# 48 late gate units of a gated encoder block: from plain to Strassen form, behind all branch projections

## The chip, the cores and the metric

One core of a Trainium2 chip runs the whole kernel. The metric is the device time of one execution in microseconds. TensorE does matmuls into PSUM (8 banks of 128 x 512 floats), VectorE (DVE) and ScalarE (ACT) work elementwise, GpSimd (POOL) here issues DMAs that add in DRAM, and SyncE (SP) issues most of the other DMAs.

## What is computed

One encoder layer over 512 tokens with 2048 features, in float32. Cut to what matters:

```python
xn = rms_norm(h, norm_mix_g[l])
...                                    # projections, two attentions: att_a, att_b (512 x 1024 each)
y_a = att_a @ w_branch_a[l]            # 1024 -> 2048
y_b = att_b @ w_branch_b[l]            # 1024 -> 2048
gates = jax.nn.sigmoid(xn @ w_gate[l]) # 2048 -> 4096
merged = gates[..., :D_MODEL] * y_a + gates[..., D_MODEL:] * y_b
h = h + merged @ w_out[l]
hn = rms_norm(h, norm_mlp_g[l])
u = jnp.square(jax.nn.relu(hn @ w_mlp_in[l]))
h = h + u @ w_mlp_out[l]
return rms_norm(h, norm_final_g)
```

## The kernel before

Every float32 product is made of three matmuls: each operand is split into a high part (rounded to the fast format float32r, by ScalarE) and a low part (the rest, by VectorE), and `product` adds high x high, high x low and low x high in PSUM (lines 1728 to 1730). All weights stream once from DRAM. A unit is one load of 512 KB of weights: four blocks of 128 rows by 256 columns. Its way is: SP loads it into one of four slots of `landing`, ScalarE makes `w_hi`, VectorE `w_lo` (`split`, two slots each), and TensorE multiplies (`features`, 24 matmuls of 512 columns). Semaphores count units: `unit_lo` (split), `unit_used` (multiplied).

The stages follow one another on TensorE:
- Stage 1, 88 units (UNITS1): query, key and value projections, with attention woven in, and the gates of the column blocks 0 and 1 of both branches (blocks "g" of BLOCKS), which stay in `side` as `gate`.
- Stage 2, 80 units, blocks B2 to B2_END + 1. For each column block nb of 256 (eight of them) there are four branch units (two of `w_branch_a`, two of `w_branch_b`, from at_hi and at_lo, the split attention outputs), and for six of the eight then four units each of the two gates of block nb + 2, from xn_hi and xn_lo (the split x times its gain; the division by the token's root mean square is applied to the result, by `gate_logits`). These are the 48 late gate units. VectorE multiplies gate and branch straight from PSUM (`scaled_a`, `merge_b`) and adds the two into `feat`.
- Stage 3, 32 units from B3: `w_out`, from the split merged features (`merged_part`), two banks in turn out of eight (`out_pair`).
- The up stage, 128 units in Strassen form. The operands are cut into 2 x 2 blocks and seven products replace eight: a unit is seven forms by two blocks by three matmuls of 256 columns, 42 matmuls. Four units make a group `s`, with its own four PSUM banks (`up_bank`), two groups in turn. SP loads four blocks of weights (`up_units`, laid out in DRAM as 4 KB a partition) into one of three slots `up_raw`, VectorE adds three more forms (`up_sums`), ScalarE and VectorE split the seven (`up_high`, `up_low`), and after a group VectorE mixes the seven products into four blocks (`first_product` on ScalarE, `mixed_products`, `fourth_block`, `hidden`). At step n VectorE does `up_low(n)`, what is due for older groups, and then `up_sums(n + 2)`, in this order; SP issues the load of unit n when `up_low(n - 3)` is done.
- The down stage, also in Strassen form.

Beside all this POOL runs 18 rounds of `totals`, which make sums of weight blocks in DRAM: two copies of 1 MB, two accumulating transfers of 1 MB, a copy, an accumulating transfer, a copy, an accumulating transfer, each step waiting for the one before. A round is released by `unit_used`:

```python
for m in range(2 + STEPS):
    pool.wait_ge(unit_used, 12 + 8 * m if m < 10 else 84 + 10 * (m - 9))
    for part in range(6):
        totals(m, part)
```

So rounds 10 to 17 start at units 6, 16, 26, ..., 76 of stage 2. The pair of accumulating transfers is `part == 1`.

## Time and profile before

| | |
|---|---|
| median of 3 runs | 2479.97 us (2479.5 to 2480.07) |
| span of the profiled execution | 2477.4 us; its own time is not listed, the median lies 2.6 us above the span |
| TensorE busy | 2460.5 us, 99% |
| VectorE, ScalarE, GpSimd busy | 1660.1, 1062.9, 193.0 us |
| stage 2 in the trace | from about 599 to 1032 us (80 units) |
| up stage in the trace | from about 1204 to 1847 us (128 units) |

The span runs from the first to the last instruction. TensorE's matmuls are pipelined and overlap in the records, so their mean duration (389 ns for 512 columns) is more than the distance between two of them; the distance is read from counts in a window. A landing of a DMA is the time from its issue to its semaphore. q0 is the DMA queue of POOL, q1 that of SP.

### The profile page before, as it was taken

How to read it: one execution, taken by the hardware profiler on the slowest of the kernel's cores; microseconds unless marked ns; L12 is line 12 of the kernel's file. 1: busy time of each engine (PE TensorE's matmuls, PEld its weight loads, DVE VectorE, ACT ScalarE, POOL GpSimd, SP SyncE). 2: the span in 40 equal slices, each digit the busy share in tenths (PEclk: the TensorE clock that was granted, in tenths of full speed). 3: DMA queues.
4: the chain of work that ended last, by engine and by line, in shares of the span. 5: the costliest groups of instructions: out<-in, count | busy, mean ns of one | idle time of the engine just before them, and what ended most of it. 6: DMA issues, size and time to landing. Idle time of an engine off the chain costs nothing.

```text
span 2477.4 us, 34658 instructions
## 1 busy us (share of the span) xinstructions
PE 2460.5 (99%) x14162; PEld 2176.6 (88%) x14162; DVE 1660.1 (67%) x2260; ACT 1062.9 (43%) x1382; POOL 193.0 (8%) x185
## 2 busy tenths in 40 slices
PE   9999999999999999999999999999999999999998
PEld 8898898898888888888999999999998888888886
DVE  6566555556333332544788888888869788877898
ACT  5566755556222222312433433333335444444445
POOL 0011000100010100101200000000001011110010
PEclk9999999999999999999999999999999999999999
DMA  7788998888898999965554434433479666566652
GB/s 262 212 254 240 237 250 244 234 251 224 231 263 246 245 251 254 257 181 151 167 191 153 135 131 131 134 128 130 135 230 336 229 230 225 190 225 232 233 191 108
DMA packets 226819, 517.11 MB, mean 209 GB/s; under 512 B 30672, under 2 KB 159840, under 8 KB 215152
## 3 DMA queue, kind: packets, MB, share of 16 engines
q1 hardware_dynamic: 213712, 363.52, 44.1%
q0 software_dynamic: 12672, 151.00, 24.3%
q8 instruction: 103, 1.69, 0.3%
q10 hardware_dynamic: 288, 0.54, 0.1%
q14 instruction: 44, 0.36, 0.0%
HBM read 489.80 MB, written 176.20 MB: 269 GB/s over the span
## 4 chain that ended last, share of the span: by engine, by line
PE 95%; DVE 3%; ACT 1%; issue 1%; DMA 0%; SPq 0%; ACTq 0%; DVEq 0%
PE bank L1728 31%; PE bank L1730 30%; PE bank L1729 30%; PE bank L1803 1%; PE bank L1838 1%; PE bank L1817 1%; DVE ring L1519 0%; DMA stream<-in_x_features 0%; DVE up_lo L1411 0%; DVE form_lo_b L1377 0%; DVE stream L1547 0%; DVE stream L1568 0%; DVE at_lo L1261 0%; ACT q_twice L752 0%; DVE stream L1559 0%
## 5 line engine op out<-in xcount | busy, mean ns | idle before, releaser
L1045 DVE TENSOR_TENSOR w_lo<-landing,w_hi 128x1024 fp32r<-128x1024 f32 x199 | 247.7, 1244 | 447.4 <-ACT w_hi L696 447.3
L1728 PE MATMUL bank<-xn_hi,w_hi 128*128 128x512 f32 x1184 | 464.7, 392 | 2.3 <-DVE w_lo L1202 1.3
L1730 PE MATMUL bank<-xn_hi,w_lo 128*128 128x512 f32 x1184 | 461.2, 390 | 0.0
L1729 PE MATMUL bank<-xn_lo,w_hi 128*128 128x512 f32 x1184 | 460.7, 389 | 0.0
L696 ACT ACTIVATE w_hi<-landing 128x1024 fp32r<-128x1024 f32 x199 | 210.9, 1060 | 575.6 <-PE bank L1730 575.2
L919 ACT ACTIVATE up_hi<-up_raw 128x1792 fp32r<-128x1792 f32 x128 | 218.1, 1704 | 401.8 <-PE bank L1730 391.5
L968 ACT ACTIVATE ring<-down_raw 128x1024 fp32r<-128x1024 f32 x224 | 237.5, 1061 | 312.4 <-PE bank L1730 312.4
L1519 DVE TENSOR_TENSOR ring<-down_raw,ring 128x1024 fp32r<-128x1024 f32 x224 | 285.4, 1284 | 68.2 <-ACT ring L968 68.0
L1411 DVE TENSOR_TENSOR up_lo<-up_raw,up_hi 128x1792 fp32r<-128x1792 f32 x128 | 259.9, 2030 | 85.2 <-ACT up_hi L919 85.2
L1728 PEld LDWEIGHTS bank<-xn_hi,w_hi 128*128 128x128 f32 x1184 | 222.4, 188 | 47.3 <-issue 3.3
L1730 PEld LDWEIGHTS bank<-xn_hi,w_lo 128*128 128x128 f32 x1184 | 222.2, 188 | 46.9
L1729 PEld LDWEIGHTS bank<-xn_lo,w_hi 128*128 128x128 f32 x1184 | 222.5, 188 | 44.9 <-issue 0.2
L1728 PE MATMUL bank<-ring,down_forms 128*128 128x512 f32 x656 | 255.5, 390 | 0.9 <-DVE ring L1519 0.9
L1729 PE MATMUL bank<-ring,down_forms 128*128 128x512 f32 x656 | 255.2, 389 | 0.0
L1730 PE MATMUL bank<-ring,down_forms 128*128 128x512 f32 x656 | 255.2, 389 | 0.0
L1728 PE MATMUL bank<-form_hi_b,up_hi 128*128 128x256 f32 x896 | 253.8, 283 | 0.4 <-DVE up_lo L1411 0.4
L1728 PE MATMUL bank<-form_hi_a,up_hi 128*128 128x256 f32 x896 | 253.6, 283 | 0.0
L1730 PE MATMUL bank<-form_hi_b,up_lo 128*128 128x256 f32 x896 | 253.6, 283 | 0.0
L1729 PE MATMUL bank<-form_lo_a,up_hi 128*128 128x256 f32 x896 | 253.6, 283 | 0.0
L1729 PE MATMUL bank<-form_lo_b,up_hi 128*128 128x256 f32 x896 | 253.6, 283 | 0.0
L1730 PE MATMUL bank<-form_hi_a,up_lo 128*128 128x256 f32 x896 | 253.6, 283 | 0.0
L1728 PEld LDWEIGHTS bank<-form_hi_b,up_hi 128*128 128x128 f32 x896 | 172.0, 192 | 0.7 <-DVE up_lo L1411 0.6
(192 smaller groups left out, 4386.4 us busy)
## 6 DMA issues: line engine op xcount, KB each, us to landing
down_totals<-in_down_blocks POOLq DMA_DIRECT2D x64, 1024.0 KB, 9.4
up_raw<-in_up_units SPq DMA_DIRECT2D x128, 512.0 KB, 3.4
down_raw<-down_totals SPq DMA_DIRECT2D x128, 512.0 KB, 4.4
down_raw<-in_down_blocks SPq DMA_DIRECT2D x96, 512.0 KB, 4.3
landing<-in_w_in SPq DMA_DIRECT2D x71, 512.0 KB, 6.2
landing<-in_w_gate SPq DMA_DIRECT2D x64, 512.0 KB, 6.3
landing<-in_w_out SPq DMA_DIRECT2D x32, 512.0 KB, 3.7
hidden_rows<-hidden_out SPq DMA_DIRECT2D x32, 512.0 KB, 3.4
```

What stands on the lines that cost most here:

```text
L696: nc.scalar.activation(w_hi[:, u % SPLIT, :], landing[:, u % LAND, :], ACT.Copy).then_inc(unit_hi, 1)
L919: nc.scalar.activation(up_hi[n % 2], up_raw[n % 3][:, 1:8, :], ACT.Copy).then_inc(up_hi_done, 1)
L968: nc.scalar.activation(ring[i % RING][:, 0, :], raw_of(i), ACT.Copy).then_inc(piece_hi, 1)
L1045: nc.vector.tensor_tensor(w_lo[:, s, :], landing[:, u % LAND, :], w_hi[:, s, :].bitcast(F32), ALU.subtract).then_inc(unit_lo, 1)
L1411: nc.vector.tensor_tensor(up_lo[n % 2], up_raw[n % 3][:, 1:8, :], up_hi[n % 2].bitcast(F32), ALU.subtract).then_inc(up_lo_done, 1)
L1519: nc.vector.tensor_tensor(part[:, 1, :], raw_of(i), part[:, 0, :].bitcast(F32), ALU.subtract)\
L1728: nc.tensor.matmul(dst, a_hi, b_hi, start=start, stop=False, **kw)
L1729: nc.tensor.matmul(dst, a_hi, b_lo, start=False, stop=False, **kw)
L1730: return nc.tensor.matmul(dst, a_lo, b_hi, start=False, stop=stop, **kw)
L1803: ins = nc.tensor.matmul(bank[:, bk, col:col + n], query[:, t * P:(t + 1) * P], keys[:, first:first + n], start=col == 0 and k == 0, stop= ...
L1817: ins = nc.tensor.transpose(bank[:, bk, col + k * P:col + (k + 1) * P], probs[:, start + k * P:start + (k + 1) * P], identity[:])
L1838: ins = nc.tensor.matmul(dst, v_parts[:, s, j, head, :], moving, start=j == 0 and part is pt_hi, stop=j == TT - 1 and part is pt_lo, skip_ ...
```

## The change

All 32 branch units come first, the 16 of branch a and then the 16 of branch b. Products of the column blocks 0 and 1 are multiplied by their gates as before (`scaled_a`, `merge_b`). Those of the six later blocks are kept (`keep_branch` on ScalarE): y_a in `feat`, y_b through two buffers into DRAM (`store_yb`), from where it comes back block by block (`load_yb`). Meanwhile x is loaded again, scaled by gain and root mean square, and made into the seven Strassen forms for each of eight feature pairs (`x_form_block`, `x_form_sums`, `x_form_high`, `x_form_low`), in three batches, the last of which waits for the end of the branch units. Then the 48 gate units run as 12 groups of four in the form of the up stage, with three slots `gate_raw`. After a group ScalarE applies the sigmoid (`open_gate`) and VectorE multiplies with y_a (even groups) or with y_b, and adds (odd groups, `through_gate`). The first w_out unit gets split buffers of its own, and three splits and the merged parts move. POOL's rounds 13 to 17 are released by gate units. The diff, cut to its core:

```diff
+KEPT = 2
+GROUPS = 2 * (D // CB - KEPT)
+GATE_UNITS = 4 * GROUPS
+GATE_ORDER = (list(IN_TURN) + [(s, v) for s in range(2, GROUPS - 2) for v in range(4)]
+              + [(GROUPS - 2 + s, v) for s, v in IN_TURN])
+X_BATCHES = (range(0, 4), range(4, 6), range(6, 8))
...
+            def load_x_forms(batch):
+
+                kps = X_BATCHES[batch]
+                sp.wait_ge(unit_used, UNITS1 + (0, BRANCH_UNITS // 2, BRANCH_UNITS)[batch])
+                for kp in kps:
+                    for i in (kp, kp + KP):
+                        slots = slice(0, 8, 7) if i < KP else slice(3, 7, 3)
+                        sp.dma_start(x_raw[kp][:, slots, :], x_blocks[:, i, :].rearrange("p (h n) -> p h n", h=2))\
+                            .then_inc(x_form_landed[batch], 16)
+
+            def store_yb(nb):
+
+                sp.wait_ge(yb_kept, nb - KEPT + 1)
+                sp.dma_start(yb_rows[nb - KEPT], yb_stage[nb % 2]).then_inc(yb_stored[nb % 2], 16)
+
+            def load_yb(nb):
+
+                if nb == KEPT:
+                    sp.wait_ge(yb_stored[0], 16 * 3)
+                sp.wait_ge(merged, nb)
+                sp.dma_start(yb_back[:], yb_rows[nb - KEPT]).then_inc(yb_landed, 16)
+
+            def load_gate(n):
+
+                s, v = GATE_ORDER[n]
+                if n == 0:
+                    sp.wait_ge(att_ready, HEADS)
+                elif n < 3:
+                    sp.wait_ge(unit_lo, UNITS1 + BRANCH_UNITS - 4 + 2 * n)
+                else:
+                    sp.wait_ge(gate_lo_done, n - 2)
+                sp.dma_start(gate_raw[n % 3][:, 0:4, :].rearrange("p b n -> p (b n)"),
+                             gate_units[s % 2 * (D // CB) + KEPT + s // 2, v]).then_inc(gate_landed[n % 3], 16)
+
+            for w in range(BRANCH_UNITS):
+                src, nb = (wba, wbb)[w // 16], w % 16 // 2
+                load(B2 + w // 4, w % 4, src[:, KU * (w % 2):KU * (w % 2 + 1), nb * CB:(nb + 1) * CB], CB)
+                if w == 6:
+                    load_x_forms(0)
+                elif w == 20:
+                    load_gate(0)
+                elif w == 22:
+                    load_x_forms(1)
+                elif w in (27, 29, 31):
+                    store_yb((w - 23) // 2)
+            load_gate(1)
+            load_gate(2)
+            load_x_forms(2)
+            for n in range(3, GATE_UNITS):
+                load_gate(n)
+                if n in (3, 4, 5):
+                    store_yb(n + 2)
+                for s in range(1, GROUPS, 2):
+                    if n == min(gate_end(s) + 2, GATE_UNITS - 1):
+                        load_yb(KEPT + s // 2)
...
+            def keep_branch(q):
+
+                m, nb = q // 8, q % 8
+                if nb < KEPT:
+                    return
+                act.wait_ge(unit_used, UNITS1 + 2 * q + 2)
+                bank_pair = bank[:, 2 * (nb % 2):2 * (nb % 2) + 2, :]
+                if m == 0:
+                    nc.scalar.activation(feat[:, 2 * nb:2 * nb + 2, :], bank_pair, ACT.Copy).then_inc(ya_kept, 1)
+                    return
+                if nb < 4:
+                    act.wait_ge(merged, KEPT)
+                else:
+                    act.wait_ge(yb_stored[nb % 2], 16 * (nb // 2 - 1))
+                nc.scalar.activation(yb_stage[nb % 2], bank_pair, ACT.Copy).then_inc(yb_kept, 1)
...
+            def gate_high(n):
+
+                act.wait_ge(gate_summed, 3 * n + 3)
+                if n == 0:
+                    act.wait_ge(merged, KEPT)
+                elif n == 1:
+                    act.wait_ge(unit_used, UNITS1 + BRANCH_UNITS)
+                else:
+                    act.wait_ge(gate_used, n - 1)
+                nc.scalar.activation(gate_hi[n % 2], gate_raw[n % 3][:, 1:8, :], ACT.Copy).then_inc(gate_hi_done, 1)
...
+            def open_gate(s):
+
+                act.wait_ge(gate_mixed, 5 * s + 5)
+                nc.scalar.activation(gate_mix[:, 0:4, :], gate_mix[:, 0:4, :], ACT.Sigmoid).then_inc(gate_open, 1)
+
+            act.wait_ge(at_lo_done, KB // 2)
+            for w in range(2, BRANCH_UNITS):
+                split(B2 + w // 4, w % 4)
+                if w >= 3 and w % 2 == 1:
+                    keep_branch((w - 3) // 2)
+                if 12 <= w < 16:
+                    x_form_high(w - 12)
+                elif w in (26, 27):
+                    x_form_high(w - 22)
+
+            for n in range(GATE_UNITS):
+                gate_high(n)
+                if n == 1:
+                    keep_branch(15)
+                elif n in (2, 3):
+                    x_form_high(n + 4)
+                if n >= 4 and GATE_ORDER[n - 4][1] == 3:
+                    open_gate(GATE_ORDER[n - 4][0])
+                if n >= 2 and GATE_ORDER[n - 2][1] == 3:
+                    gate_first_product(GATE_ORDER[n - 2][0])
...
+            def x_form_block(kp):
+
+                batch = x_batch(kp)
+                dve.wait_ge(x_form_landed[batch], 16 * 2 * len(X_BATCHES[batch]))
...
+            def through_gate(s):
+
+                nb = KEPT + s // 2
+                dve.wait_ge(gate_open, s + 1)
+                if s % 2 == 0:
+                    dve.wait_ge(ya_kept, nb - KEPT + 1)
+                    nc.vector.tensor_tensor(feat_blocks(nb), feat_blocks(nb), gate_blocks, ALU.mult).then_inc(gated, 1)
+                    return
+                dve.wait_ge(yb_landed, 16 * (nb - KEPT + 1))
+                nc.vector.tensor_tensor(gate_blocks, gate_blocks, yb_blocks, ALU.mult).then_inc(branch_b, 1)
+                dve.wait_ge(branch_b, nb + 1)
+                dve.wait_ge(gated, s // 2 + 1)
+                nc.vector.tensor_tensor(feat_blocks(nb), feat_blocks(nb), gate_blocks, ALU.add)\
+                    .then_inc(merged, 1)
+                dve.wait_ge(merged, nb + 1)
...
+            for n in range(GATE_UNITS):
+                gate_low(n)
+                if n == 1:
+                    x_form_block(6)
+                    x_form_block(7)
+                    x_form_sums(2)
+                elif n in (3, 4):
+                    x_form_low(n + 3)
+                if n >= 4 and GATE_ORDER[n - 4][1] == 3:
+                    through_gate(GATE_ORDER[n - 4][0])
+                if n >= 2 and GATE_ORDER[n - 2][1] == 3:
+                    mixed_gate(GATE_ORDER[n - 2][0])
+                if n >= 3 and GATE_ORDER[n - 3][1] == 3:
+                    fourth_gate(GATE_ORDER[n - 3][0])
+                if n + 2 < GATE_UNITS:
+                    gate_sums(n + 2)
...
+            fourth_gate(GROUPS - 2)
             merged_part(0)
-            split(B2_END, 2)
             merged_part(1)
-            split(B2_END, 3)
-            scaled_a(B2_END, 0, NBR - 2)
+            split(B3, 0)
             merged_part(2)
...
+            merged_part(3)
+            through_gate(GROUPS - 2)
+            mixed_gate(GROUPS - 1)
+            fourth_gate(GROUPS - 1)
+            split(B3, 1)
...
             for m in range(2 + STEPS):
-                pool.wait_ge(unit_used, 12 + 8 * m if m < 10 else 84 + 10 * (m - 9))
+                if m < 13:
+                    pool.wait_ge(unit_used, 12 + 8 * m if m < 10 else 84 + 10 * (m - 9))
+                else:
+                    pool.wait_ge(gate_used, (4, 14, 25, 36, 47)[m - 13])
...
+            def gate_unit(n, s, v):
+
+                pe.wait_ge(gate_lo_done, n + 1)
+                if v == 0 and s == 0:
+                    pe.wait_ge(att_ready, HEADS)
+                elif v == 0 and s == 1:
+                    pe.wait_ge(yb_kept, 6)
+                elif v == 0:
+                    pe.wait_ge(gate_mixed, 5 * (s - 1))
```

## Rows read from the trace of the kernel before

**Rows 1.** The page: span, busy shares, granted clock, the chain that ended last.

```profile
span 2477.4 us, 34658 instructions
PE 2460.5 (99%) x14162; PEld 2176.6 (88%) x14162; DVE 1660.1 (67%) x2260; ACT 1062.9 (43%) x1382; POOL 193.0 (8%) x185
...
PE 95%; DVE 3%; ACT 1%; issue 1%; DMA 0%; SPq 0%; ACTq 0%; DVEq 0%
```

**Rows 2.** Waits of TensorE: whole span's longest, then all from 590 to 1260 us.

```profile
PE bank L1728 <- DVE w_lo L1202: 1.3, 1, 1.3
...
PE bank L1728 <- DVE up_lo L1411: 0.4, 1, 0.4
PE bank L1728 <- DVE w_lo L1045: 0.2, 1, 0.2
```

**Rows 3.** Windows: length, busy (count) of PE, PEld, DVE, ACT, POOL; clock, DMA share, GB/s.

```profile
744.00:806.00 62.00, 62.00 (x275) 51.32 (x274) 18.48 (x16) 13.79 (x13) 6.88 (x10) 1.00 0.88 250
1426.00:1488.00 62.00, 62.00 (x519) 62.00 (x518) 54.04 (x75) 24.80 (x24) 0.00 (x0) 1.00 0.40 131
```

**Rows 4.** Timeline of SP: start, length, issues; 795 to 828 and 638 to 650.

```profile
797.90 27.47 SPq L501 DMA_DIRECT2D landing<-in_w_gate  x6
...
640.06 5.86 SPq L501 DMA_DIRECT2D landing<-in_w_branch_a  x2
```

**Rows 5.** Timeline of ScalarE in the up stage: two splits.

```profile
1406.25 1.70 ACT L919 ACTIVATE up_hi<-up_raw 128x1792 fp32r<-128x1792 f32 x1 [2.73 <-PE bank L1730]
...
1411.29 1.70 ACT L919 ACTIVATE up_hi<-up_raw 128x1792 fp32r<-128x1792 f32 x1 [2.73 <-PE bank L1730]
```

**Rows 6.** Timeline at the start of stage 2: VectorE, ScalarE, TensorE.

```profile
604.18 4.62 DVE L1261 TENSOR_TENSOR at_lo<-stream,at_hi 128x1024 fp32r<-128x1024 f32 x4
...
606.38 1.04 ACT L696 ACTIVATE w_hi<-landing 128x1024 fp32r<-128x1024 f32 x1
...
609.99 0.50 PE L1728 MATMUL bank<-at_hi,w_hi 128*128 128x512 f32 x1 [0.21 <-DVE w_lo L1045]
```

**Rows 7.** Timeline of VectorE in the up stage: low part, mixing, sums, low part.

```profile
1413.03 2.02 DVE L1411 TENSOR_TENSOR up_lo<-up_raw,up_hi 128x1792 fp32r<-128x1792 f32 x1 [1.50 <-ACT up_hi L919]
1414.97 0.68 DVE L1425 TENSOR_TENSOR mix<-bank,first_term 128x512 f32<-128x512 f32 x1
...
1417.09 0.68 DVE L1400 TENSOR_TENSOR up_raw<-up_raw 128x512 f32<-128x512 f32 x1
...
1418.60 2.02 DVE L1411 TENSOR_TENSOR up_lo<-up_raw,up_hi 128x1792 fp32r<-128x1792 f32 x1
```

**Rows 8.** Landings: landing 620 to 1054 us; up_raw; the load of 645.55.

```profile
DMA to landing us min/median/max: 3.3/5.9/13.3
...
DMA to landing us min/median/max: 3.1/3.4/7.9
...
landing<-in_w_branch_a SPq DMA_DIRECT2D x1, 512.0 KB, 12.4
```

**Rows 9.** DMA queues by window (packets, MB, share): 650:653; 656:659; 667:672; 1410:1415 us.

```profile
q0 software_dynamic: 74, 0.57, 91.4%
q1 hardware_dynamic: 75, 0.08, 9.3%
...
q1 hardware_dynamic: 998, 0.99, 99.3%
...
q1 hardware_dynamic: 16, 0.02, 1.2%
...
q1 hardware_dynamic: 144, 0.52, 30.1%
```

**Rows 10.** Timeline of POOL in round 10: trigger, accumulating pair, third accumulating transfer.

```profile
632.38 1.01 POOL L1663 DMA_DIRECT2D down_totals<-in_down_blocks  x2 [20.65 <-PE bank L1730]
641.17 1.74 POOL L1666 DMA_DIRECT2D down_totals<-in_down_blocks  x2 [7.77 <-DMA down_totals<-in_down_blocks]
...
664.95 0.80 POOL L1666 DMA_DIRECT2D down_totals<-in_down_blocks  x1 [7.03 <-DMA down_totals<-down_totals]
```

More of the change, by code:

```diff
@@ L92, in up_place, with gate_end, x_batch @@
     return UP_ORDER.index((s, v))
+def gate_end(s):
+    return GATE_ORDER.index((s, 3))
+def x_batch(kp):
+    return next(b for b, kps in enumerate(X_BATCHES) if kp in kps)
 def summed_in_dram(n):
@@ new lines, in x_form_block @@
+            def x_form_block(kp):
+                batch = x_batch(kp)
+                dve.wait_ge(x_form_landed[batch], 16 * 2 * len(X_BATCHES[batch]))
+                for i in (kp, kp + KP):
+                    slots = slice(0, 8, 7) if i < KP else slice(3, 7, 3)
+                    nc.vector.scalar_tensor_tensor(
+                        out=x_raw[kp][:, slots, :], in0=x_raw[kp][:, slots, :], scalar=gains[:, 0, i:i + 1],
+                        in1=rms_row[:].rearrange("p (h n) -> p h n", h=2), op0=ALU.mult, op1=ALU.mult)\
+                        .then_inc(x_form_raw, 1)
@@ new lines, in _ @@
+            for w in range(2, BRANCH_UNITS):
+                split(B2 + w // 4, w % 4)
+                if w in (3, 5):
+                    scaled_a((w - 3) // 2)
+                elif w in (19, 21):
+                    merge_b((w - 19) // 2)
+                if 8 <= w < 12:
+                    x_form_block(w - 8)
+                elif w == 12:
+                    x_form_sums(0)
+                elif 13 <= w < 17:
+                    x_form_low(w - 13)
+                elif w in (24, 25):
+                    x_form_block(w - 20)
+                elif w == 26:
+                    x_form_sums(1)
+                elif w in (27, 28):
+                    x_form_low(w - 23)
+                elif w == 30:
+                    gate_sums(0)
@@ L1381, in _ @@
                 for u in range(KU):
[L1382 to L1384 removed]
+                    if n or u == 3:
+                        split(B3 + n, u)
+                    if n == 0 and u == 2:
                         merged_part(NBR - 1)
@@ L1879, in gate_block @@
-            def gate_block(b, pair, left):
-                pe.wait_ge(branch_b if pair else branch_a, left)
-                for u in range(4):
-                    features(b, u, 2 * pair, KU * u, u == 0, u == 3, xn_hi, xn_lo)
-            with pe.Fori(0, LOOP2) as i:
-                for j in range(2):
-                    b = i * PER2 + (B2 + 3 * j)
-                    nb = i * 2 + j
-                    branches(b, nb)
-                    gate_block(b + 1, 0, nb + 1)
-                    gate_block(b + 2, 1, nb + 1)
@@ L1892, in _, with branch @@
-            branches(B2_END, NBR - 2)
-            pe.wait_ge(branch_a, NBR - 1)
-            for u in range(2):
-                features(B2_END + 1, u, 0, KU * u, u == 0, u == 1, at_hi, at_lo)
-            pe.wait_ge(branch_b, NBR - 1)
-            for u in range(2):
-                features(B2_END + 1, 2 + u, 2, KB // 2 + KU * u, u == 0, u == 1, at_hi, at_lo)
+            def branch(w):
+                m, nb, half = w // 16, w % 16 // 2, w % 2
+                pe.wait_ge(at_lo_done, 4 * m + 2 * half + 2)
+                if half == 0 and m == 0 and nb < KEPT:
+                    pe.wait_ge(scaled_ready, N_BLOCKS1 - 1 + nb)
+                elif half == 0 and nb < KEPT:
+                    pe.wait_ge(ya_kept, 5 + nb)
+                elif half == 0 and nb < 4:
+                    pe.wait_ge((branch_a, branch_b)[m], nb - 1)
+                elif half == 0:
+                    pe.wait_ge((ya_kept, yb_kept)[m], nb - 3)
+                features(B2 + w // 4, w % 4, 2 * (nb % 2), KU * half, half == 0, half == 1, at_hi[m], at_lo[m])
```

325 lines of the change are left out of this document (203 added, 122 removed).

## The prediction

> **What bounds the kernel now.** I read the page first: TensorE is busy in 2460.5 of 2477.4 us at its full clock, and the chain that ended last is 95% TensorE [rows 1]. The view of waits then says that this busy time is nearly free of holes: from 590 to 1260 us, which holds all the work that the change touches, TensorE waits twice, 0.6 us in all [rows 2]. So the time is the number of matmuls times their pace, and the question is what the new form gives back in pace and what it newly makes TensorE wait for. The windows give both paces: in a stretch of branch and gate units 62 us hold 275 matmuls of 512 columns (225.5 ns each), in the up stage, whose form the change copies, 62 us hold 519 of 256 columns (119.5 ns) [rows 3]. DVE is the other thing to see there: 18.5 of 62 us in the gate stretch, 54.0 in the up stage. VectorE goes from idle to nearly the bound.
>
> **The gain.** A gate unit before is 24 matmuls of 512 columns. SP issues one load per unit: six issues span 27.47 us, less the issue's own 0.37, over five gaps: 5.42 us a unit [rows 4]. In the new form a unit is 42 matmuls of 256 columns; ScalarE's splits of the up stage start every 5.04 us [rows 5]. 48 units x 0.38 us = 18.2 us less, if none waits. (From the paces [rows 3] it is 18.9; I take the spacings, where no missing record counts.) The 32 branch units only change order.
>
> **Entry into the stage.** ScalarE now waits for all of at_lo before it splits branch unit 2. Before, it split at 606.38, and at_lo ended at 608.80; VectorE's half followed at once and TensorE resumed at 609.99 [rows 6]. Now: 608.85 + 1.04 (ScalarE's row) + 1.2 (VectorE, 4.62 for four of this size), about 611.1. Cost 1.2 us with the handoffs. The moved branch units, scaled_a, merge_b and the copies that keep a branch have two bank pairs in turn and ScalarE and VectorE mostly idle beside them (13.8 and 18.5 of 62 us [rows 3]); stores of y_b (512 KB, bound by the loads' 3.3 to 13.3 us to landing [rows 8]) have two units or more each. I cost these at nothing; without that cover a unit's copy would be some 1.1 us. The x loads are wanted four units later at the least.
>
> **Steady pace of the gate groups.** From the up stage [rows 5, 7], with S the start of a unit on TensorE (where ScalarE's split starts): ScalarE splits the next unit S to S+1.70, VectorE subtracts S+1.74 to S+3.7, and TensorE wants it at S+5.04, so the slack is about 1.3 us. VectorE's effective costs (start to start) are 1.94 for the low part, 1.52 for the three sums, 2.12 for the four mixing steps. The heaviest new step, an odd group's passage through its gate, has two dependent operations over 1024 columns, 1.16 each back to back [rows 6], which I set at 2.5 us with the waits between and behind them: 1.94 + 2.5 + 1.52 = 5.96, and the next subtraction starts 0.9 late, inside the slack. So the pace holds, when data are there.
>
> **Start of the gate stage.** Call E the end of the last branch unit. The last forms of x (features 6 and 7) take memory that the branches read until E, so SP issues their four loads (1 MB) at E, and VectorE stands at them before it comes to unit 2. If nothing else is moving they land about E+6 (four issues of 0.4, then the 2 us of lead and 3.1 us for 1024 packets at the 333 a microsecond that q1 reaches alone: 998 packets in 3 us [rows 9]). Behind them: four products and four sums of 128x512 (0.68 each and a handoff, 2.8 and 2.8), the three sums of unit 3 (1.52), the subtraction (2.0): 9.1 us [rows 7]. Unit 2 then starts at E+15.1 where TensorE wants it at E+10.1: 5.0 us. But a round of POOL's totals is running: its trigger is 6 units before E, and its third accumulating transfer starts 32.6 us after the trigger (632.38 to 664.95), which is E [rows 10]. For five microseconds such a transfer leaves q1 next to nothing (16 packets) [rows 9]; with that the loads land near E+9 and the hold-up is 8 to 9. ScalarE's chain (it waits for a store of y_b queued behind those loads, then 1.06 + 1.70) ends about E+15 and is covered by VectorE's. I take 7.5, bounds 5 and 10.
>
> **POOL's rounds against a shorter lead.** This is the largest term, and the least certain. Before, a unit's load had four landing slots; now it has three and VectorE must reach it one step earlier, for the sums. Load n is issued when the subtraction of unit n-3 ends, at S(n-4)+3.85; behind its landing stand sums 1.52 and the subtraction of unit n-1, 2.0, due at S(n-4)+15.1. So a landing may take 7.7 us without cost; beyond, TensorE waits the difference. In the up stage landings are 3.4 (median; POOL quiet); in the gate stage of before 3.3 to 13.3 [rows 8]. The long ones have a pattern: POOL's two accumulating transfers at 641.17 held up the load issued at 645.55 for 12.4 us, until 658.0, 25.5 after the trigger at 632.38 [rows 4, 8, 10]. It starves for 4 us, then its 1 KB packets go one for one with POOL's 8 KB packets, 75 against 74 in 3 us, until POOL is done [rows 9]. The new loads come in 4 KB packets (144 for 0.52 MB in 5 us of the up stage [rows 9]), 128 instead of 512, so one for one they need about 5 to 6 us: first packet at 17.5, landed at about 24.1 after the trigger. The rounds keep their triggers (gate units 4, 14, 25, 36, 47, at a unit's start), and the load that falls into the gap is issued at trigger + 10.1 + 3.85 = 13.9: 10.2 us to landing, 2.5 over the 7.7. In the rounds at 4 and 36 a load of y_b (512 KB more) is queued ahead of it: 1.4 us more, 3.9. Four rounds (that of unit 47 meets w_out's loads, four slots): 2.5 + 2.5 + 3.9 + 3.9 = 12.8. After such a hold-up VectorE has no slack left, and a heavy step next to it costs again: in round one the step with a passage, a mixing and sums (1.94 + 1.2 + 2.12 + 1.52 = 6.8 against 5.04) 1.7, in round two an odd passage 0.9: 2.6, taken as 2.5. The term is 15.3 us; its bounds are 0 (landings under 7.7) and 21 (landed as late as before's: 25.5 - 13.9 = 11.6, 3.9 over, with the y_b load ahead 5.3: 2 x 3.9 + 2 x 5.3 + 2.5).
>
> The Trainium skill ("DMA: Bandwidth & Descriptors", section "Queues, rings and completion order") says that each DMA engine takes turns between its queues packet by packet; the 75 against 74 agree. By that rule the size of packets decides, which speaks for 10.2 rather than 11.6. It doesn't enter the sum otherwise.
>
> **End of the gate stage.** VectorE has after the last subtraction: mixing, fourth block, seven merged parts, passage and mixing of the last group, three splits. Counted from the start of unit 46, out unit 1 gets its split at 16.8 (3.7 low part, 2.12 + 0.4, four merged parts and a split at 1.14, passage 1.14, mixing 2.1 and 0.4, split 1.14), wanted at 10.1 + 5.4 = 15.5: 1.3 us. The first and third out units are ready in time.
>
> **Sum.** -18.2 + 1.2 + 7.5 + 15.3 + 1.3 = +7.1 us on the profiled span 2477.4. The span lies 2.6 below the median of the runs, which I carry over: 2479.97 + 7.1 = 2487.1, slower by 0.29%.
>
> **Rivals.**
> 1. *Landings under 7.7 us (other side).* 4 KB packets get through POOL's, or the load that matters just misses the two transfers. The rounds cost nothing, the start 5: -18.2 + 1.2 + 5 + 1.3 = -10.7, 2469.3. For it: the up stage's 3.4 with the same packets. Against: there POOL moves nothing; and 4 us pass before even the first packet. It decides at 7.7 us of landing in the four rounds. With the start at 7.5 it is 2471.8. Chance 0.30.
> 2. *Half of it.* Landings of 9: 1.3 us in a round, 5 in all, start 7.5, no second step: -3.2, 2476.8; up to 2483 with the second steps. No measurable change. Chance 0.17.
> 3. *Worse: landings as before's, or a clock that falls.* The rounds at 21, the start at 9: +14.3, 2494.3. And the longest wait of TensorE that the view lists is 1.3 us [rows 2]; now it would wait 7.5. The granted clock is 1.00 [rows 3], the 2.4 GHz level. Were it to fall to 1.2 GHz after the five hold-ups, with half a unit lost each time (2.5 us, an estimate from the 5.04 of [rows 5]), 12.5 us come on top of the forecast: 2499.6. Chance 0.12. The Trainium skill ("TensorE: Matmul & The Clock Gate", section "Why this matters for your kernels") warns that gaps of idleness between bursts bring the half clock; no row here shows it either way.
> 4. *The forecast*, 2481 to 2494: chance 0.41.
>
> That the new form doesn't save time on TensorE isn't open: the pace of both forms is measured side by side.
>
> **Range and chances.** Nothing under 0.2% (5 us) can be told from no change. Slower by more: the forecast, its lower edge cut off, and rival 3: 0.52. Faster: 0.29. Between: 0.19. The range runs from just under rival 1 to between rival 3's two prices, 2468 to 2497; the forecast's own is 2481 to 2494.
>
> **What would show it.** Right: in windows of the gate stage without a hold-up 42 matmuls per 5.04 us; TensorE waits on gate_lo after unit 1 (5 to 10 us, VectorE at x_raw's products waiting for a DMA), and once in each round, at units 9, 19, 30 and 41, 2 to 4 us, with VectorE's sums released by the DMA into gate_raw; a longest landing of gate_raw near 10. Wrong: gate_raw landings all under 8, a stage without waits, or waits that follow mixing or passage steps without a late landing, which would mean that VectorE is the bound. What I trust least is how 4 KB packets share with POOL's.

## The result, and the profile after

The changed kernel takes 2516.36 us (median of 4 runs, 2512.95 to 2519.13) against 2479.73 (2478.96 to 2480.07) beside it: the ratio is 1.0148, 95% interval 1.0134 to 1.0163. It is slower by 1.48%, 36.6 us, where 7.1 were forecast and the range ended at 2497. The page of the profiled run, with the lines that answer to [rows 1]; the lines under its first two are the chain that ended last, by engine and by line:

```profile
span 2511.1 us, 36310 instructions
PE 2456.8 (98%) x15026; PEld 2212.7 (88%) x15026; DVE 1817.5 (72%) x2488; ACT 1119.4 (45%) x1414; POOL 193.5 (8%) x185
...
PE 84%; DVE 7%; DMA 5%; ACT 1%; issue 1%; SPq 0%; DVEq 0%; ACTq 0%
PE bank L2017 27%; PE bank L2019 27%; PE bank L2018 27%; DMA gate_raw<-in_gate_units 4%; DVE gate_lo L1511 2%; PE bank L2092 1%; PE bank L2127 1%; PE bank L2106 1%; DVE gate_raw L1501 1%; DMA stream<-in_x_features 0%; DMA x_raw_c<-in_x_features 0%; DVE ring L1805 0%; DVE up_lo L1697 0%; DVE gate_raw L1504 0%; ACT gate_hi L1019 0%
```

TensorE's busy time hardly moved, the span grew by 33.7 us, and 4% of the chain is now the transfer into gate_raw, where transfers had rounded to 0 (a transfer's whole flight counts in the chain, work beside it too, so this isn't yet the loss). The waits say the same from both sides: first TensorE's longest over the whole span (total, times, longest; [rows 2] had one of 1.3 and next to nothing around the gate), then, from 590 to 1080 us, what VectorE and ScalarE stood at:

```profile
PE bank L2017 <- DVE gate_lo L1511: 34.3, 15, 10.9
PE bank L2017 <- DVE w_lo L1231: 2.5, 3, 1.5
...
DVE gate_raw L1501 <- DMA gate_raw<-in_gate_units: 53.5, 17, 5.7
ACT gate_mix L1003 <- DMA yb_rows<-gate_mix: 12.8, 1, 12.8
...
DVE x_raw_c L1471 <- DMA x_raw_c<-in_x_features: 8.2, 1, 8.2
```

TensorE waits for the low part of a gate unit 15 times. VectorE, which makes it, was held 17 times by a load (line 1501 is the first of a unit's three sums). TensorE's 10.9 us are the start of the stage; its other 14 waits, 23.4 us, are what VectorE's slack leaves of the 53.5 that it stood at loads.

Windows of the gate stage (columns as in [rows 3]):

```profile
790.00:810.00 20.00, 13.23 (x89) 13.23 (x90) 17.05 (x19) 9.50 (x7) 0.92 (x2) 0.69 0.63 171
810.00:830.00 20.00, 19.74 (x165) 19.54 (x163) 16.39 (x22) 6.93 (x6) 2.63 (x4) 1.00 0.94 285
830.00:850.00 20.00, 16.52 (x121) 16.14 (x122) 14.63 (x20) 7.10 (x6) 1.34 (x2) 0.91 0.84 213
...
890.00:910.00 20.00, 17.19 (x131) 16.99 (x130) 15.11 (x19) 6.64 (x6) 1.85 (x3) 0.91 0.82 226
...
1010.00:1030.00 20.00, 18.38 (x138) 18.18 (x137) 14.02 (x19) 5.50 (x5) 1.32 (x2) 0.90 0.91 246
```

At full pace (42 in 5.04 us) such a window would hold 167 matmuls; 165 are in the second, 121 and 131 in others. The granted clock shows a second loss, 0.69, 0.91, 0.91, 0.90: it falls behind the longer waits. Where each microsecond went comes out of TensorE's timeline, counting 42 matmuls to a unit from the start of each. Gap is the extra time ahead of a unit's first matmul:

```
stage: unit 0 at 775.7, unit 2 at 796.77 (gap 11.1), unit 47 at 1061.46, end 1066.5
gaps at unit: 8 0.6, 9 3.3, 12 1.5, 15 1.3, 19 3.0, 25 3.0, 28 0.7, 29 3.1, 30 0.4,
              36 0.9, 38 4.1, 40 1.8, 43 1.1, 44 0.8, 46 0.7      (others 5.04 a unit)
half clock:   796.77-802.47 (26 matmuls, 0.213 us apart behind the first), 840.05-843.45 (16), 898.16-901.36 (15),
              932.23-935.62 (16), 1009.06-1014.12 (23)
```

From unit 2 to unit 47 pass 264.7 us where 45 x 5.04 is 226.8: 37.9 too many. The five half-clock stretches are 20.8 us long and hold 96 matmuls, which take 11.5 at 0.1195: 9.3 lost. The listed gaps make 26.3, and smaller ones the rest, 2.3. With the start the account closes: -18.2 (gain) + 11.1 + 37.9 + 1.3 + 0.4 (two gaps among the branch units) + 0.9 (end) = 33.4 of 33.7.

### The profile page after: what moved, and what is told of

It is laid out like the page before. It is cut to its first block, busy times and chain, and to the rows that moved or that the text cites. A ratio compares the mean times of both kernels' runs of the same rounds, so it can differ in the third digit from the quotient of the medians.

```text
span 2511.1 us, 36310 instructions
## 1 busy us (share of the span) xinstructions
PE 2456.8 (98%) x15026; PEld 2212.7 (88%) x15026; DVE 1817.5 (72%) x2488; ACT 1119.4 (45%) x1414; POOL 193.5 (8%) x185
## 4 chain that ended last, share of the span: by engine, by line
PE 84%; DVE 7%; DMA 5%; ACT 1%; issue 1%; SPq 0%; DVEq 0%; ACTq 0%
PE bank L2017 27%; PE bank L2019 27%; PE bank L2018 27%; DMA gate_raw<-in_gate_units 4%; DVE gate_lo L1511 2%; PE bank L2092 1%; PE bank L2127 1%; PE bank L2106 1%; DVE gate_raw L1501 1%; DMA stream<-in_x_features 0%; DMA x_raw_c<-in_x_features 0%; DVE ring L1805 0%; DVE up_lo L1697 0%; DVE gate_raw L1504 0%; ACT gate_hi L1019 0%
## 5 line engine op out<-in xcount | busy, mean ns | idle before, releaser
L1231 DVE TENSOR_TENSOR w_lo<-landing,w_hi 128x1024 fp32r<-128x1024 f32 x150 | 187.4, 1250 | 248.6 <-ACT w_hi L835 248.5
L835 ACT ACTIVATE w_hi<-landing 128x1024 fp32r<-128x1024 f32 x150 | 158.9, 1059 | 374.1 <-PE bank L2019 363.7
L2017 PE MATMUL bank<-xn_hi,w_hi 128*128 128x512 f32 x792 | 312.4, 394 | 3.0 <-DVE w_lo L1387 1.3
L2019 PE MATMUL bank<-xn_hi,w_lo 128*128 128x512 f32 x792 | 308.8, 390 | 0.0
L2018 PE MATMUL bank<-xn_lo,w_hi 128*128 128x512 f32 x792 | 308.3, 389 | 0.0
L2017 PEld LDWEIGHTS bank<-xn_hi,w_hi 128*128 128x128 f32 x792 | 148.8, 188 | 33.5 <-issue 4.4
L2019 PEld LDWEIGHTS bank<-xn_hi,w_lo 128*128 128x128 f32 x792 | 148.7, 188 | 31.7
L2018 PEld LDWEIGHTS bank<-xn_lo,w_hi 128*128 128x128 f32 x792 | 148.9, 188 | 29.6 <-issue 0.2
L2017 PEld LDWEIGHTS bank<-form_hi_a,up_hi 128*128 128x128 f32 x896 | 172.0, 192 | 0.8 <-DVE up_lo L1697 0.8
```

What stands on the lines that cost most here:

```text
L835: nc.scalar.activation(hi, landing[:, u % LAND, :], ACT.Copy).then_inc(unit_hi, 1)
L1231: nc.vector.tensor_tensor(lo, landing[:, u % LAND, :], hi.bitcast(F32), ALU.subtract).then_inc(unit_lo, 1)
L2017: nc.tensor.matmul(dst, a_hi, b_hi, start=start, stop=False, **kw)
L2018: nc.tensor.matmul(dst, a_hi, b_lo, start=False, stop=False, **kw)
L2019: return nc.tensor.matmul(dst, a_lo, b_hi, start=False, stop=stop, **kw)
```

## The experiments

Each was timed beside the kernel of before on the same chip; ratios are against that kernel, whose medians there were 2479.62 (first four), 2479.21 (next four) and 2479.14 (last four). The changed kernel was timed apart from them, so a difference from it is taken between what each has over its own kernel of before (36.6 us for the change).

### POOL's late rounds left out, in both kernels

POOL runs 18 rounds of block totals for the down stage; rounds 12 to 17 lie beside the gate stage. Both kernels leave them out, and down steps 10 to 15 read plain blocks in place of those sums, so nothing else moves.

```diff
-                src = down_blocks[m // 2, m % 2, BLOCK_OF[j]] if j in BLOCK_OF else down_totals[m // 2, m % 2, SUM_OF[j]]
+                src = down_blocks[m // 2, m % 2, {**BLOCK_OF, **SUM_OF}[j]] if j in BLOCK_OF or m >= 10 else down_totals[m // 2, m % 2, SUM_OF[j]]
...
-            sp.wait_ge(totals_added, 16 * 4 * (2 + STEPS))
+            sp.wait_ge(totals_added, 16 * 4 * 12)
...
-            for m in range(2 + STEPS):
+            for m in range(12):
```

(The edit is the same in both kernels.)

> The changed kernel with POOL's rounds 12 to 17 left out (the down stage reads plain weight blocks in place of the sums of steps 10 to 15, so that part of the computation is changed, with the same bytes). Theory 1 (POOL's transfers make the loads late, lateness makes TensorE wait, waits lower its clock): the 25.8 us of waits behind unit 2 in the gate stage go down to under 3, the half-clock stretches behind them (four, 6.7 us lost) vanish, landings of gate_raw stay under 7; the start still waits, for 1 MB of x, some 5 to 9 us instead of 11.1, with one half-clock stretch. Time 2470 to 2476. Rival (VectorE is the bound of the gate stage: its steps with mixing and passage don't fit into 5.04 us): waits at the heavy steps stay, 10 us or more behind unit 2, time over 2490.

> Control: the kernel before with the same rounds 12 to 17 left out (same change of the computation). If what the left-out rounds cost before is nothing, as its view of waits says (0.6 us of waits in this stage), the time stays within 1 us of 2479.7. Should it fall by several us as well, the gain of the run above isn't the gate stage's alone.

The changed kernel took 2474.16 us (2472.59 to 2477.75, 10 runs), ratio 0.9979 [0.9969, 0.9989]. The one of before took 2479.45, ratio 0.9999 [0.999, 1.0009]. The same six rounds cost the new form 42.2 us and the old one 0.2. TensorE's waits for the low part, the landings of gate_raw, and the windows, without the rounds:

```profile
PE bank L2017 <- DVE gate_lo L1511: 6.2, 2, 5.4
...
DMA to landing us min/median/max: 3.4/3.7/14.1
...
790.00:810.00 20.00, 18.58 (x140) 18.58 (x141) 16.94 (x18) 8.37 (x6) 0.00 (x0) 0.86 0.41 118
810.00:830.00 20.00, 20.00 (x168) 19.99 (x168) 17.05 (x22) 8.09 (x8) 0.00 (x0) 1.00 0.45 136
```

168 matmuls in 20 us are four units of 5.0: the gain is there. What stays is unit 2 (gap 5.6, then 18 matmuls at half clock, 791.42 to 795.42), and unit 10, 0.9 late, where VectorE meets a passage, a mixing and sums in one step. So VectorE is not the bound, and the loss comes with the rounds. That they cost the form with four landing slots next to nothing points at the lead that loads now have; the runs below try that.

### Unread matmuls keep the clock up

The changed kernel, with matmuls whose results nobody reads ahead of six waits: 85 before unit 2, 24 each before units 9, 19, 25, 29 and 38.

```diff
+                for _ in range({2: 85, 9: 24, 19: 24, 25: 24, 29: 24, 38: 24}.get(n, 0)):
+                    nc.tensor.matmul(up_products(s if n > 2 else 0, 7, 8)[:, 0, :], x_hi[0][:, 0, 0:P],
+                                     x_hi[0][:, 0, :], start=False, stop=False, skip_group_check=True)
                 pe.wait_ge(gate_lo_done, n + 1)
```

> The changed kernel with matmuls that nobody reads (256 columns each, into the unused eighth half bank) ahead of the waits of units 2 (85 of them), 9, 19, 25, 29 and 38 (24 each), so that TensorE works through most of each long wait. Theory 1: the waits end when they did, the five stretches at 1.2 GHz (20.8 us long, 9.3 us lost) vanish, time 2505 to 2510. Rival (the slow stretches are not due to idleness, or the time is anyway given by the loads and VectorE, so a faster clock is only waited away): 2513 or more.

2515.89 us (2512.68 to 2525.01), ratio 1.0158 [1.0138, 1.0177]: no gain, as the rival had it. Yet the mean clock went from 0.992 to 0.997 and the stretches at half clock from five to two (799.03 to 802.40 and 976.62 to 979.82). The window of the second hold-up has full clock now:

```profile
830.00:850.00 20.00, 17.30 (x140) 16.73 (x140) 14.53 (x20) 7.38 (x6) 1.34 (x2) 1.00 0.75 207
```

From unit 3 to unit 47 it took 255.3 us against 257.1. The rival's reason, that a faster clock is only waited away, is not shown by this, because the unread matmuls had a price of their own. They were set for the waits of one execution, and in this one two of those waits were short or missing. At unit 25 (VectorE's timeline, then TensorE's):

```profile
928.53 2.02 DVE L1511 TENSOR_TENSOR gate_lo<-gate_raw,gate_hi 128x1792 fp32r<-128x1792 f32 x1
...
929.67 3.04 PE L2174 MATMUL bank<-x_hi_a 128*128 128x256 f32 x24
932.55 0.28 PE L2017 MATMUL bank<-x_hi_a,gate_hi 128*128 128x256 f32 x1
```

The low part was ready at 930.5 and TensorE came to it at 932.55, 2.0 late; ahead of unit 38 it was ready before the 24 began, and they cost 2.9. These 4.9 us are about what the clock gave back behind unit 2: one stretch that loses 1.5 us instead of four that lose 6.7. And unit 2's gap grew from 11.1 to 14.1 us, since here a load into gate_raw came late as well. So whether the clock's 9.3 us could be had in the changed kernel stays open.

### The start of the stage alone

Two stores of y_b and the load of unit 3 go ahead of the x loads, and the forms of features 6 and 7 are made behind unit 3.

```diff
             load_gate(2)
+            store_yb(5)
+            load_gate(3)
+            store_yb(6)
             load_x_forms(2)
-            for n in range(3, GATE_UNITS):
+            for n in range(4, GATE_UNITS):
...
-                if n == 1:
+                if n == 3:
                     x_form_block(6)
                     x_form_block(7)
                     x_form_sums(2)
```

> The changed kernel with the start of the gate stage in another order: stores 5 and 6 of y_b and the load of unit 3 ahead of the x loads of the last batch, and that batch's products and sums on VectorE behind the low part of unit 3 instead of unit 1. Theory 1 with two chains at the start (VectorE behind the x loads, ScalarE behind a store of y_b, the second 1.7 us shorter): the 11.1 us before unit 2 go to under 2, new waits of 2 to 4 us come before units 4 and 5, no half-clock stretch at the start: 8 us less, 2505 to 2511. Rival (the start is bound by VectorE's work, which is only moved): 2513 to 2517.

2513.35 us (2505.83 to 2514.17), ratio 1.0136 [1.0119, 1.0153], some 3 us below the change, with intervals that overlap: the rival's range. The profiled execution was the fastest of the four, 2505.83. In it unit 2 has no wait, but units 4, 5 and 7 have 3.6, 0.9 and 3.2 of it, the first and the last with half clock behind them. From the start of the stage to unit 8 it takes 52.4 us instead of 54.6. So most of the start's cost is only moved, and 2.2 us of it are saved; the rest of that execution's lead came later, from unit 8 to unit 47 (226.0 us instead of 231.3), where nothing was changed.

### The rounds moved into the down stage

Nothing is left out. Rounds 12 to 17 run one by one behind the block sums of the odd down steps 1 to 11, and SP waits for a step's totals before it loads them.

```diff
+                if m % 2 == 1 and 12 + m // 2 < 2 + STEPS:
+                    for part in range(6):
+                        totals(12 + m // 2, part)
...
                 sp.wait_ge(piece_lo, i - RAW_SLOTS + 1)
+                if p == 0:
+                    sp.wait_ge(totals_added, 16 * 4 * (m + 3))
                 load_raw(i)
```

> The changed kernel, all work kept, with POOL's rounds 12 to 17 moved into the down stage (one behind the block sums of each odd step from 1 to 11; SP waits for the round of a step before its first load). Theory 1: the gate stage looks as with the rounds left out (2474.2), and the down stage, whose loads have twelve slots, hides the rounds: 2472 to 2478. Rival: the down stage's own loads (SP's queue 190 GB/s there) collide with the rounds and TensorE waits for piece_lo: 2485 or more.

2473.71 us (2470.82 to 2476.97, 10 runs), ratio 0.9977 [0.9968, 0.9987]: the same as without the rounds, and 42 us below the changed kernel. The down stage takes them for nothing, though its 16 DMA engines are then busy to 0.94 and 0.99 (0.65 and 0.64 in the same windows of before); these windows of it have no hole on TensorE:

```profile
1900.00:2000.00 100.00, 100.00 (x443) 82.81 (x442) 86.88 (x86) 52.33 (x51) 24.35 (x17) 1.00 0.94 314
2100.00:2200.00 100.00, 100.00 (x443) 82.81 (x442) 79.86 (x81) 45.15 (x45) 17.82 (x16) 1.00 0.99 338
```

So this much traffic doesn't cost TensorE anything by itself. The down ring has 12 landing slots, gate_raw three, which fits the lead as what decides; the two stages differ in more than that, and a fourth slot for gate_raw was not tried.

### More lead for the loads: the sums one step later

The sums of a unit stand one step later in VectorE's order, which gives a landing one unit more. Run on the changed kernel, with the other start, and with the other start and the moved rounds.

```diff
                 gate_low(n)
+                if n >= 2 and n + 1 < GATE_UNITS:
+                    gate_sums(n + 1)
...
-                if n + 2 < GATE_UNITS:
-                    gate_sums(n + 2)
+                if n == 0:
+                    gate_sums(2)
```

> The changed kernel with VectorE's three sums of a unit one step later (behind the low part of unit n come the sums of unit n + 1, not of n + 2), rounds where they were. The late load then blocks nothing until one unit later: by the prediction's working the landing that costs nothing rises from 7.7 to about 12 us. Theory 1 with the lead as the weak point: the landings stay (longest near 10.7), but the 25.8 us of waits behind unit 2 fall to under 6, only the start stays: 2487 to 2496. Rival (the DMA engines' throughput is the bound, whatever the order): waits move to other units, 2508 or more.

> The run before with the start in its other order as well (stores 5 and 6 and the load of unit 3 ahead of the x loads, the last forms of x behind unit 3). Theory 1: the start's 11 us go down to 3 to 6, in pieces short enough to keep the clock: 2480 to 2489. Rival (start's cost is only moved): as the run before.

> All three: rounds moved to the down stage, sums one step later, start in its other order. Theory 1: only VectorE's own work at the start is left (1 to 4 us), with 1.7 at the entry and 1 at the end: 2479.7 - 18.2 + 4 to 7 = 2465 to 2469. Rival (a floor of VectorE in the gate stage shows once the loads are in time): 2472 or more.

2501.70 us (2497.94 to 2504.97), ratio 1.0086 [1.0069, 1.0103]; with the start 2495.76 (1.0069 [1.0052, 1.0086]); with all three 2489.54 (1.0040 [1.0026, 1.0055]). All three lie above what I had expected (2487 to 2496, 2480 to 2489, 2465 to 2469). VectorE's waits for the loads from 800 to 1060 us, in the first of them, have nearly gone:

```profile
DVE gate_lo L1511 <- ACT gate_hi L1019: 42.0, 29, 1.8
DVE gate_raw L1501 <- DMA gate_raw<-in_gate_units: 5.3, 3, 2.4
```

The rounds are the same, and one unit more of lead takes these waits away: that is the runs' best evidence for the lead, though the units also come slower now. The first line is what took their place, and the last expectation missed it. VectorE's and ScalarE's timeline of the third kernel, in a step with nothing else to do:

```profile
864.47 2.02 DVE L1517 TENSOR_TENSOR gate_lo<-gate_raw,gate_hi 128x1792 fp32r<-128x1792 f32 x1 [0.63 <-ACT gate_hi L1024]
866.41 0.68 DVE L1507 TENSOR_TENSOR gate_raw<-gate_raw 128x512 f32<-128x512 f32 x1
868.05 1.70 ACT L1024 ACTIVATE gate_hi<-gate_raw 128x1792 fp32r<-128x1792 f32 x1 [3.61 <-DVE gate_raw L1512]
869.78 2.02 DVE L1517 TENSOR_TENSOR gate_lo<-gate_raw,gate_hi 128x1792 fp32r<-128x1792 f32 x1 [1.77 <-ACT gate_hi L1024]
```

Low part (1.94), sums of the next unit (1.64), its split (1.73) and the next low part now form one ring: 5.31 us a unit, 0.27 over TensorE's 5.04. Steps with a mixing or a passage take longer still (5.6 and 6.0 us from one low part to the next), so that units 8 to 47 take 5.49 us each. A kernel further down differs from this one in the sums alone (the other start with the rounds moved, 2470.22): the later sums cost 19.3 us there, more than the 18.2 that the new form gains. Where the rounds stay they are still worth having (14 us).

### Smaller packets in POOL's accumulating transfers

If packets take turns, POOL's of 4 KB instead of 8 should let the loads through sooner.

```diff
-    accum_op=ALU.add, max_dma_last_dim=8192
+    accum_op=ALU.add, max_dma_last_dim=4096
```

> The changed kernel with POOL's accumulating transfers cut into packets of at most 4 KB instead of 8 KB, nothing else. Theory 1 with turns packet by packet: a gate load of 128 packets of 4 KB that goes one for one with them loses half as much to them; the longest landings of gate_raw fall from 10.7 to about 8 to 9, the waits behind unit 2 from 25.8 to 10 to 15 us, time 2500 to 2508. Rival (what counts is the time until the first packet, some 4 us, or the bytes queued by POOL, not the size of a packet): landings stay at 10 to 11, time within 3 us of 2516.4.

2510.77 us (2506.71 to 2513.42), ratio 1.0127 [1.0111, 1.0142]: 5 us better than the change, with intervals that just overlap, between the expectations. Longest landing and median are 13.2 and 6.1 (14.3 and 6.3), and the long waits came at units 2, 20, 31 and 41 instead. Behind the start the longest landings are 12.4 to 12.9 us, where the change has 10.4 to 10.8: they didn't fall to 8 or 9, as theory 1 had it. What this says of turn-taking stays open.

### What is left, with the rounds moved

Three kernels on top of the moved rounds: 45 unread matmuls ahead of unit 2; the other start; and that start with ScalarE's wait for all of at_lo put off from branch unit 2 to unit 8.

```diff
-            act.wait_ge(at_lo_done, KB // 2)
             for w in range(2, BRANCH_UNITS):
                 split(B2 + w // 4, w % 4)
+                if w == 7:
+                    act.wait_ge(at_lo_done, KB // 2)
```

> The kernel with the rounds moved to the down stage (2473.7), with 45 unread matmuls of 256 columns ahead of the wait of unit 2. There the wait of 5.7 us is the stage's only long one and 4 us at 1.2 GHz follow it. Theory 1: the stretch vanishes, unit 2 lasts 5.04 instead of 7.2 us, and as no late load follows, all of the 1.8 to 2.2 us is gained (2471.7, at the edge of what the runs tell; the profile shows it). Rival, as the unread matmuls in the changed kernel showed: it is waited away behind the next units and the start of unit 10 relative to the stage's start is the same.

> Rounds moved to the down stage and the start in its other order, sums where they were (two units ahead). Theory 1, after the run in which sums one unit ahead closed a ring of 1.94 + 1.52 + 1.75 = 5.3 us: units keep 5.04 us, the start costs about 4 instead of 5.7 + 2: 2470 to 2472. Rival (the other order fits only with late sums): 2474 or more.

> As the run before, and ScalarE waits for at_lo only ahead of its first write into feat (behind the split of branch unit 7) instead of ahead of that of unit 2. Theory 1: the 1.5 us of wait at branch unit 2 goes, 2469 to 2471; if it was hidden anyway, the same as the run before.

The unread matmuls: 2470.76 us (2469.95 to 2471.57), ratio 0.9966 [0.9953, 0.9979], some 3 less than the moved rounds, with intervals that overlap; the profile is the better witness. TensorE's first matmul of unit 2 there:

```profile
791.27 0.39 PE L2019 MATMUL bank<-x_hi_a,gate_hi 128*128 128x256 f32 x1 [0.39 <-DVE gate_lo L1513]
791.49 0.28 PE L2020 MATMUL bank<-x_lo_a,gate_hi 128*128 128x256 f32 x1
791.61 0.28 PE L2021 MATMUL bank<-x_hi_a,gate_lo 128*128 128x256 f32 x1
791.73 0.28 PE L2019 MATMUL bank<-x_hi_a,gate_hi 128*128 128x256 f32 x1
```

0.12 apart from the second on; unit 2 lasts 5.14 us and not 7.23, and from unit 3 to unit 47 both kernels take 223.0. So here, with nothing to wait for behind it, the 2 us of the clock can be had. The other start: 2470.22 (2469.63 to 2471.81), ratio 0.9965 [0.9952, 0.9979]; it removes the wait at unit 2, gets one of 2.8 at unit 4 and the half clock behind it (28 matmuls, 798.19 to 804.33). The last: 2469.46 (2468.73 to 2470.20), ratio 0.9961 [0.9947, 0.9975]. The gap at the entry is 0.69 us instead of 1.90. It is the fastest kernel here: 9.7 us below before, 46 below the change; its interval overlaps those of the two runs ahead of it.

## Why the prediction was wrong

**Direction and mechanism held.** The gate stage has its gain of 0.38 us a unit wherever a unit has its data; TensorE waits on gate_lo after unit 1 and then for loads that met POOL's pairs, at units 9, 19, 29 and 40 (forecast 9, 19, 30 and 41) for 3.3, 3.0, 3.1 and 1.8 us (2.5 or 3.9 each), 11.2 in all where 12.8 were forecast. Those loads landed about when it was worked out that they would. Two answers on DMA issues of the changed kernel, from 824 to 826.5 and from 859 to 861.5 us (last number: us to landing):

```profile
gate_raw<-in_gate_units SPq DMA_DIRECT2D x1, 512.0 KB, 10.8
...
gate_raw<-in_gate_units SPq DMA_DIRECT2D x1, 512.0 KB, 9.5
```

The first is a load that meets the pair: 10.8 (10.4, 10.6 and 10.5 in the next three rounds) against 10.2. And the queues of 888 to 889 us (packets, MB, share):

```profile
q0 software_dynamic: 20, 0.16, 78.5%
q1 hardware_dynamic: 19, 0.08, 20.5%
```

One for one with POOL's packets, as the 1 KB packets did in [rows 9], and 4 KB each. What I had trusted least was right. That 10.2 came so near is luck in part: a first packet at 17.5 and 5 to 6 us of packets make 22.5 to 23.5 after the trigger, 8.6 to 9.6 to landing, and no row stands for the rest of the way to 24.1. In the round of 867.8 the first packet came 18.2 after the trigger, and it took 7.8 more to landing.

**The step that failed** is the term "POOL's rounds", 15.3 us with a bound of 21. Behind unit 2's own stretch (2.6 us) it measured 35.3: 28.6 of gaps and 6.7 of half clock. It priced one load in each round, the one that meets the pair, and took every other accumulating transfer and copy at nothing. The loads that it priced cost 11.2 of the 26.3 us of listed gaps; the other 15.1, with 2.3 of small gaps and the 6.7 of half clock, it did not have (1.3 of all this is there without the rounds too). The second row above is such a load: issued beside a single accumulating transfer, it landed after 9.5 us. Nine loads from unit 3 on were issued up to 4 us behind the start of a single one, and took 6.8 to 10.4 us, five of them 8.0 or more, over the 7.7 that a landing may take. The longest wait behind the start, 4.1 us at unit 38, came from neither: its load was issued at 994.6, together with the two copies that open a round, and took 10.7. VectorE's timeline and POOL's put it side by side:

```profile
829.64 0.42 DVE L1540 TENSOR_TENSOR gate_mix<-bank,gate_mix 128x256 f32<-128x256 f32 x1
835.01 0.69 DVE L1501 TENSOR_TENSOR gate_raw<-gate_raw 128x512 f32<-128x512 f32 x1 [4.96 <-DMA gate_raw<-in_gate_units]
...
870.10 0.69 DVE L1501 TENSOR_TENSOR gate_raw<-gate_raw 128x512 f32<-128x512 f32 x1 [3.44 <-DMA gate_raw<-in_gate_units]
...
893.33 0.69 DVE L1501 TENSOR_TENSOR gate_raw<-gate_raw 128x512 f32<-128x512 f32 x1 [4.57 <-DMA gate_raw<-in_gate_units]
```

```profile
819.76 1.72 POOL L1952 DMA_DIRECT2D down_totals<-in_down_blocks  x2 [8.85 <-DMA down_totals<-in_down_blocks]
...
857.64 0.81 POOL L1952 DMA_DIRECT2D down_totals<-in_down_blocks  x1 [5.33 <-DMA down_totals<-down_totals]
```

The pair of 819.76 holds VectorE until 835.01 (TensorE 3.3), the single transfer of 857.64 holds it until 870.10 (TensorE 1.3). VectorE stood at a load 17 times, not four. The trace of before had it to be seen. Asked one by one, 20 of its loads from 620 to 1000 us took 8.1 us or more, and the longest of all met no pair: it was issued at 901.18 behind a single accumulating transfer, and the next pair came when it had landed (POOL, the landing, POOL):

```profile
897.95 0.81 POOL L1666 DMA_DIRECT2D down_totals<-in_down_blocks  x1 [6.41 <-DMA down_totals<-down_totals]
...
landing<-in_w_branch_a SPq DMA_DIRECT2D x1, 512.0 KB, 13.3
...
914.47 1.74 POOL L1666 DMA_DIRECT2D down_totals<-in_down_blocks  x2 [9.07 <-DMA down_totals<-in_down_blocks]
```

I looked up one round's pair and took the median for the rest.

**The start.** 7.5 forecast (5 to 10), 11.1 measured, and 2.6 of half clock behind it. Without the rounds it is 5.6, forecast 5.0 for quiet queues, so that part's working holds. Beside them the x loads landed not at E+9 but at E+12:

```profile
787.86 2.74 DVE L1471 SCALAR_TENSOR_TENSOR x_raw_c<-x_raw_c,gains,rms_row 128x512 f32<-128x512 f32 x4 [8.21 <-DMA x_raw_c<-in_x_features]
...
794.69 2.02 DVE L1511 TENSOR_TENSOR gate_lo<-gate_raw,gate_hi 128x1792 fp32r<-128x1792 f32 x1
```

```profile
790.43 1.02 ACT L1003 ACTIVATE gate_mix<-bank 128x1024 f32<-128x1024 f32 x1 [12.84 <-DMA yb_rows<-gate_mix]
791.35 1.69 ACT L1019 ACTIVATE gate_hi<-gate_raw 128x1792 fp32r<-128x1792 f32 x1
```

```profile
776.13 0.83 POOL L1952 DMA_DIRECT2D down_totals<-in_down_blocks  x1 [5.33 <-DMA down_totals<-down_totals]
```

POOL's third accumulating transfer did start at E, as [rows 10] had said. ScalarE's chain, which I held to be covered, ended at 793.0 against VectorE's 794.7; covered, but by 1.7 us only, so that VectorE's part alone isn't worth more.

**The clock** was half of rival 3, at 0.12, and came five times as that rival has it, behind each wait of 3 us or more bar the one at unit 29 (3.1); in the kernel with the unread matmuls a wait of 2.0, ahead of unit 32, brought it too. Its estimate was 12.5 us for five, measured are 9.3. Even both halves of that rival together, 2494.3 and 12.5, end at 2506.8: no rival had the loads that the term left out. [rows 2, 3] didn't show it since before has no such wait. The Trainium skill ("TensorE: Matmul & The Clock Gate", section "Why this matters for your kernels") had the warning, and the trace agrees. That it adds to the waits, as the rival had it, is shown with the rounds moved (2.1 us at unit 2 in the profile); for the change itself the runs leave it open.

**The small terms** held: the entry 1.2, measured 1.3, and 0.4 ahead of the matmul at 672.18 that I had at nothing; the end 1.3, measured 0.9; a heavy step 0.9 late at unit 10 without the rounds. The balance without the rounds is -18.2 + 1.7 + 5.6 + 2 + 0.9 and 1.8 at the end, -6.2; both kernels without them differ by 5.3 in their medians and by 6.8 in their profiled spans. The change by itself is a small gain. Rival 2's upper price, 2483, doesn't follow from its terms: 2476.8 and the second steps' 2.5 make 2479.3.

**What stays open:** why long waits come where they do within a round (a stall shifts the next load into the next transfer, and the units at which they fell changed from kernel to kernel); that each of the others belongs to one transfer was read from their landings, not tried with one kind of transfer at a time, and the copies' part rests on one load. Whether a fourth landing slot, which would lengthen the lead without the ring, would do was not tried. Why halving POOL's packets gave so little was not found.

## What to carry to other kernels

When a change shortens the lead of a stage's loads, work out the time that a landing may take and compare it with every landing of the old trace, each priced, not with the median and one pattern. Run first the two kernels with the background traffic left out, before and after: here that told at once 0.2 us from 42. Then move that traffic beside the stage with the deepest ring before you move work on the engine, since each step that gives the loads more lead may close a ring of its own (here 5.3 us against 5.04).

## What the runs showed of the hardware

- A 512 KB load of 4 KB packets lands in 3.7 us (median) with POOL's late rounds left out, in 10.4 to 10.8 beside two accumulating transfers of 1 MB (four loads) and in 6.8 to 10.4 beside one (nine loads). After an issue at 883.4 its queue moved next to nothing until 886 (three packets under 512 B at once), and from 887 to 892 it moved 19 to 22 packets a microsecond to POOL's 20 to 23.
- Halving the packets of the accumulating transfers took 5 us off the kernel, at the edge of what the runs tell, and left the median landing at 6.1 (6.3 before).
- In the down stage, with 12 landing slots, 16 DMA engines busy to 0.94 and 0.99 cost TensorE nothing. In the gate stage, with three, where its windows show 0.63 to 0.94, the rounds cost 42 us.
- Of four waits of 3.0 to 3.3 us, at units 9, 19, 25 and 29, the first three brought 15 or 16 matmuls at the 1.2 GHz level, beginning 0.5 to 1.4 us after work was resumed, and the last none; the waits of 4.1 and 11.1 brought 23 and 26, from the first matmul on. In the kernel with unread matmuls one of 2.0 brought 16, from 0.4 us on.
